# Seven gate and up tiles taken row by row, residual rows on VectorE alone, squares added by halves, and expert query rows made inside the second output projection

## The reference, cut to what matters

```
h = h + rmsnorm(hybrid_mixer(rmsnorm(h, g_pre_mix)), g_post_mix)
x = rmsnorm(h, g_pre_ffn)
g = causal_dwconv(x @ w_gate, w_conv)                # width 3 over tokens, D_FF = 5632
h = h + rmsnorm((silu(g) * (x @ w_up)) @ w_down, g_post_ffn)
# second block
p = rmsnorm_2(h, norm_mix_g) @ w_in                  # latents, keys, queries, gates
merged = gate_a * (o_a @ w_branch_a) + gate_b * (o_b @ w_branch_b)
h = h + merged @ w_out
h = h + peer_ffn(rmsnorm_2(h, norm_ffn_g))           # starts with x @ w_q, then top-k, experts
```

## Time and profile before

| | |
|---|---|
| median of the runs | 3484.07 us |
| profiled execution, its own time | 3487.23 us |
| its span, first to last instruction | 3485.4 us |
| TensorE (PE) busy | 3411.9 us, 98% |
| VectorE (DVE) busy | 2247.9 us, 64% |
| ScalarE (ACT) busy | 1644.5 us, 47% |
| GpSimd (POOL) busy | 120.7 us, 3% |
| HBM read | 586.71 MB, 170 GB/s |

### The profile page before, as it was taken

How to read it: one execution, slowest core, us unless ns; L and a number is a source line. 1 busy time by engine, 2 the same in 40 slices (tenths; PEclk the granted TensorE clock), 3 DMA queues, 4 the chain that set the end, 5 groups by cost and what they waited for, 6 DMA issues and landing times.

```text
span 3485.4 us, 60213 instructions
## 1 busy us (share of the span) xinstructions
PE 3411.9 (98%) x24920; PEld 3216.9 (92%) x24920; DVE 2247.9 (64%) x3715; ACT 1644.5 (47%) x2552; POOL 120.7 (3%) x173
## 2 busy tenths in 40 slices
PE   8999979999999989999999999999999999999998
PEld 8999979999999978999999999999999998887887
DVE  8775366666654467765575688877755555555655
ACT  5454444444444444444454544566644444444544
POOL 0000120000000020000000000022100000000000
PEclk9999989999999989999999999999999999999999
DMA  5433435555556634454565555544455555556654
GB/s 201 134 121 119 157 112 182 182 185 182 186 183 189 187 123 149 151 161 140 164 188 187 182 182 189 184 146 146 148 184 187 187 186 187 188 189 222 188 188 161
DMA packets 163712, 594.83 MB, mean 171 GB/s; under 512 B 18416, under 2 KB 19184, under 8 KB 163056
## 3 DMA queue, kind: packets, MB, share of 16 engines
q1 hardware_dynamic: 163440, 590.98, 53.0%
HBM read 586.71 MB, written 4.19 MB: 170 GB/s over the span
## 4 chain that ended last, share of the span: by engine, by line
PE 93%; DVE 4%; ACT 1%; DMA 1%; issue 0%; SPq 0%; ACTq 0%; DVEq 0%
PE ps L651 29%; PE ps L653 29%; PE ps L652 29%; PE ps L1086 2%; DVE wl L1158 1%; DVE tmp L1174 1%; PE ps L718 1%; ACT wh L1861 0%; DVE xl L1167 0%; PE ps L913 0%; DMA raw<-in_peer_v 0%; PE ps L894 0%; PE ps L760 0%; ACT xh L1867 0%; DVE ht L1190 0%
## 5 line engine op out<-in xcount | busy, mean ns | idle before, releaser
L1158 DVE TENSOR_TENSOR wl<-raw,wh 128x1024 fp32r<-128x1024 f32 x1114 | 1349.0, 1215 | 603.0 <-ACT wh L1861 599.9
L1861 ACT CAST wh<-raw 128x1024 fp32r<-128x1024 f32 x1114 | 1158.5, 1044 | 1029.0 <-PE ps L653 1025.6
L651 PE MATMUL ps<-xh,wh 128*128 128x256 f32 (+2 forms) x5248 | 1515.7, 289 | 47.6 <-DVE xl L1167 27.1
L653 PE MATMUL ps<-xh,wl 128*128 128x256 f32 (+2 forms) x5248 | 1496.3, 285 | 0.0
L652 PE MATMUL ps<-xl,wh 128*128 128x256 f32 (+2 forms) x5248 | 1494.4, 285 | 0.0
L651 PEld LDWEIGHTS ps<-xh,wh 128*128 128x128 f32 x5248 | 1005.8, 192 | 62.1 <-DVE xl L1167 18.3
L652 PEld LDWEIGHTS ps<-xl,wh 128*128 128x128 f32 x5248 | 1004.4, 191 | 2.3
L653 PEld LDWEIGHTS ps<-xh,wl 128*128 128x128 f32 x5248 | 1005.7, 192 | 0.0
L651 PE MATMUL ps<-wh,ch 128*128 128x512 f32 x1024 | 408.4, 399 | 0.6 <-DVE cl L1798 0.6
L653 PE MATMUL ps<-wh,cl 128*128 128x512 f32 x1024 | 403.4, 394 | 0.0
L652 PE MATMUL ps<-wl,ch 128*128 128x512 f32 x1024 | 401.6, 392 | 0.0
(11 more groups left out here) (339 smaller groups left out, 3163.2 us busy)
## 6 DMA issues: line engine op xcount, KB each, us to landing
raw<-in_peer_u SPq DMA_DIRECT2D x256, 512.0 KB, 4.2
raw<-in_peer_v SPq DMA_DIRECT2D x256, 512.0 KB, 4.4
raw<-in_w_in SPq DMA_DIRECT2D x208, 512.0 KB, 3.8
raw<-in_w_gate SPq DMA_DIRECT2D x88, 512.0 KB, 4.4
raw<-in_w_up SPq DMA_DIRECT2D x88, 512.0 KB, 4.6
raw<-in_w_down SPq DMA_DIRECT2D x80, 512.0 KB, 3.8
raw<-in_w_out SPq DMA_DIRECT2D x64, 512.0 KB, 4.3
raw<-in_w_branch_a SPq DMA_DIRECT2D x16, 512.0 KB, 3.6
```

Of the source, the lines that this page charges most:

```text
L651: t.matmul(o, lh, rh, start=start, stop=False)
L653: return t.matmul(o, ll, rh, start=False, stop=stop)
L1158: v.tensor_tensor(wl[:, i % SN, 0:cols(i)], raw[:, i % RN, 0:cols(i)], wh[:, i % SN, 0:cols(i)].bitcast(F32), ALU.subtract).then_inc(lo, 1)
L1861: s.copy(wh[:, i % SN, 0:cols(i)], raw[:, i % RN, 0:cols(i)]).then_inc(hi, 1)
```

## The change

It has five parts. The diff shows their core.

1. Gate and up tiles 0 to 6 get chunks of their own (`guk`): chunk k holds row k of all seven tiles, 128 x 896 numbers. TensorE takes the seven tiles together, 21 matmuls for each row, into seven banks; banks go round over eight instead of four. VectorE makes residual rows two ahead of the low rows. What is read from the finished tiles stands in a table `SIDESG` of slots (one slot per chunk) instead of behind every second chunk, and the first tap goes to ScalarE.
2. `post_row` does all rows on VectorE; GpSimd's `post_rows` is gone. Before the second input, the residual row k + 1 stands ahead of the low row k.
3. `sum_rows` adds the 16 squared rows as three additions of four rows and one of two, in place; TensorE sums the two rows left. This holds for all four norms of this kind.
4. ScalarE squares a finished tile before it copies it.
5. The high and low rows for the expert queries, and their squares, are made in the second output projection, each when its residual row is done. The first two expert query tiles are no longer taken as a pair.

```diff
-PLAN += _pairs("gu", 2 * FT)
+
+ROWS = 7
+PLAN += [("guk", k, 0) for k in range(KT)] + [("gu", n, c) for n in range(ROWS, 2 * FT) for c in range(2)]
...
-PLAN += _pairs("wq", 8)
+PLAN += [("wq", m, c) for m in range(8) for c in range(2)]
...
+def _sidesg():
+
+    at = [[] for _ in range(DN - GU + 8)]
+    b = KT
+    for f in range(FT):
+        b = max(b, 4 * f + 4 if f > 3 else 0)
+        if f == FT - 1:
+            b = 4 * f + 2
+        at[b] += [("g", f)]
+        at[b + 1] += [("conv", f)]
+        at[b + 2] += [("u", f), ("um", f)]
+        at[b + 3] += [("al", f)]
+        b += 2 if f % 2 else 1
+    return at
...
-        og = [ps[n % 4][:, 0:TQ if n % 2 == 0 else S] for n in range(2 * FT)]
+        def og(n):
+            return ps[n % 8][:, 0:TQ if n % 2 == 0 else S]
+
         xg = [halves(TQ), halves(S, 2)]
-        pair(GU, og[0:2], xg, 1)
-        for n in range(2, 2 * FT):
-            if n >= 4:
-                t.wait_ge(ev_gu, n - 3)
+        t.wait_ge(o_ev, 16)
+        for k in range(KT):
+            taken(GU + k)
+            t.wait_ge(xlo, 16 + k + 1)
+            for n in range(ROWS):
+                c = slice(128 * n, 128 * n + 128)
+                last = three(og(n), wh[:, (GU + k) % SN, c], wl[:, (GU + k) % SN, c], *xg[n % 2](k),
+                             k == 0, k == KT - 1)
+            last.then_inc(gemm, 1)
+            if k == KT - 2:
+                t.wait_ge(ms_add, 2)
+                mean_squares(ps[7][:, 0:TQ], [mt[:, 0, 0:TQ], mt[:, 1, 0:TQ]])
+        for n in range(ROWS, 2 * FT):
+            if n == 7:
+                t.wait_ge(ms, RMS.index("x2") + 1)
+            else:
+                t.wait_ge(ev_gu, READG.index(n - 8) + 1)
             for c in range(2):
-                chunk(GU + 2 * n + c, og[n], 8 * c, 8, xg[n % 2], c == 0, c == 1)
-            if n == 2:
-                t.wait_ge(ms_add, 4)
-                mean_squares(ps[7][:, 0:TQ], [tmp[:, 0, 0:TQ], tmp[:, 1, 0:TQ]])
+                chunk(AT["gu", n, c], og(n), 8 * c, 8, xg[n % 2], c == 0, c == 1)
...
-        pair(WQ, [ps[0][:, 0:S], ps[1][:, 0:S]], [x3, x3], 3)
-        for m in range(2, 8):
-            if m >= 4:
+        for m in range(8):
+            if m < 4:
+                t.wait_ge(res2, 12 + m + 1)
+            else:
                 t.wait_ge(qp_ok, m - 3)
             for c in range(2):
-                chunk(WQ + 2 * m + c, ps[m % 4][:, 0:S], 8 * c, 8, x3, c == 0, c == 1)
-            if m == 2:
-                t.wait_ge(ms_add, 8)
-                mean_squares(ps[7][:, 0:S], [tmp[:, 0, 0:S], tmp[:, 1, 0:S]])
+                chunk(WQ + 2 * m + c, ps[m % 4][:, 0:S], 8 * c, 8, x3, c == 0, c == 1,
+                      (lambda k: t.wait_ge(xlo, 48 + k + 1)) if m == 0 else None)
+                if (m, c) == (1, 0):
+                    t.wait_ge(ms_add, 4)
+                    mean_squares(ps[7][:, 0:S], [gate[:, 16, :], gate[:, 17, :]])
...
-        def half_sums(norm, sq_, T):
-
-            for g in range(2):
-                v.wait_ge(ms_sq, 4 * norm + 2 * g + 2)
-                v.tensor_reduce(tmp[:, g, 0:T], sq_[:, 8 * g:8 * g + 8, 0:T].rearrange("p k t -> p t k"), AX.X,
-                                ALU.add).then_inc(ms_add, 1)
+        def sum_rows(norm, rows, T, part):
+
+            if part < 3:
+                v.wait_ge(ms_sq, 4 * norm + part + 2)
+            if part:
+                v.wait_ge(own.sem, own.n)
+            if part < 3:
+                a, b = rows[:, 0:4, 0:T], rows[:, 4 * part + 4:4 * part + 8, 0:T]
+                v.tensor_tensor(a, a, b, ALU.add).then_inc(own.up(), 1)
+            else:
+                a, b = rows[:, 0:2, 0:T], rows[:, 2:4, 0:T]
+                v.tensor_tensor(a, a, b, ALU.add).then_inc(ms_add, 1)
...
-            if k % 2 == 0:
-                v.tensor_tensor(mt_[:, k, 0:T], mt_[:, k, 0:T], tmp[:, 4, 0:T], ALU.mult).then_inc(own.up(), 1)
-                v.wait_ge(own.sem, own.n)
-                v.tensor_tensor(ht[:, k, c0:c0 + T], ht[:, k, c0:c0 + T], mt_[:, k, 0:T], ALU.add).then_inc(res_v, 1)
+            v.tensor_tensor(mt_[:, k, 0:T], mt_[:, k, 0:T], tmp[:, 4, 0:T], ALU.mult).then_inc(own.up(), 1)
+            v.wait_ge(own.sem, own.n)
+            v.tensor_tensor(ht[:, k, c0:c0 + T], ht[:, k, c0:c0 + T], mt_[:, k, 0:T], ALU.add).then_inc(res_v, 1)
...
+        v.wait_ge(o_ev, 16)
+        post_row(0, mt, TQ, Q0)
+        post_row(1, mt, TQ, Q0)
+        low_row(1, 0, Q0, TQ, "g_pre_ffn")
+        post_row(2, mt, TQ, Q0)
+        low_row(1, 1, Q0, TQ, "g_pre_ffn")
+        for k in range(KT):
+            cut(GU + k + 2)
+            if k + 3 < KT:
+                post_row(k + 3, mt, TQ, Q0)
+            if k + 2 < KT:
+                low_row(1, k + 2, Q0, TQ, "g_pre_ffn")
+            if k in (6, 10, 13):
+                sum_rows(1, mt, TQ, (6, 10, 13).index(k))
+            if k == 13:
+                sum_rows(1, mt, TQ, 3)
+            if k == 14:
+                inverse_root("x2", ps[7][:, 0:TQ], D, EPS, rstd[:, 0:TQ])
...
-                v.tensor_scalar(c1, g1[:, 0:S], w[0], None, ALU.mult).then_inc(own.up(), 1)
-                v.wait_ge(own.sem, own.n)
+                v.wait_ge(gu_t, f + 1)
...
+        for slot in range(KT, DN - GU):
+            for name, f in SIDESG[slot]:
+                side_g(name, f)
             cut(GU + slot + 2)
...
+        v.wait_ge(o_ev, 32)
+        post_row(0, mt2, S, NM)
         for what, k in RAMP:
             if what == "x":
-                post_row(k, mt2, S, NM)
+                if k + 1 < KT:
+                    post_row(k + 1, mt2, S, NM)
...
+            if m:
+                low_row(3, m - 1, NM, S, "norm_ffn_g_2")
+            if m in (9, 13):
+                sum_rows(3, gate[:, 16:32, :], S, m // 4 - 2)
...
-            s.activation(mt_[:, m, 0:T], o, ACT.Copy, scale=pc(gain_name, m))
...
             s.activation(dst, o, ACT.Square).then_inc(o_sq, 1)
+            s.activation(mt_[:, m, 0:T], o, ACT.Copy, scale=pc(gain_name, m)).then_inc(o_ev, 1)
...
+        cut(GU + 2)
+        for k in range(-3, KT):
+            if k >= 0:
+                cut(GU + k + 3)
+            if k + 3 < KT:
+                s.wait_ge(res_v, k + 4)
+                high_row(1, k + 3, Q0, TQ, "g_pre_ffn")
+            if k in (0, 4, 8, 12):
+                squares_of(mt, Q0, TQ, k // 4)
+            if k == 14:
+                root("x2", rstd[:, 0:TQ])
...
+                s.wait_ge(ev_gu, READG.index(2 * f) + 1)
+                if f >= 2:
+                    s.wait_ge(gu_m, f - 1)
+                s.activation(c1, g_t[:, f % 2, 0:S], ACT.Copy, scale=pc("w_ffn_conv", 3 * f)).then_inc(gu_t, 1)
...
+        for m in range(16):
+            cut(O2 + 2 * m + 2)
+            cut(O2 + 2 * m + 3)
+            s.wait_ge(res2, m + 1)
+            high_row(3, m, NM, S, "norm_ffn_g_2")
+            if m == 3:
+                s.wait_ge(mg_l, 16)
+            if m % 4 == 3:
+                squares_of(gate[:, 16:32, :], NM, S, m // 4)
...
-        post_rows("post1", mt, TQ, Q0)
...
```

175 lines of the change are left out of this document (74 added, 101 removed).

## The result

The changed kernel takes 3455.88 us (median of four runs, 3451.66 to 3460.89), the kernel before 3483.91 (four runs, 3482.2 to 3485.85): ratio 0.992, 95% interval 0.9903 to 0.9937. The profiled execution took 3456.49 us, span 3453.8, 31.6 less than the span of before.

The account below looks back on a forecast made before the run. TensorE, busy 98% of the span, bounds the kernel; only its standstills and half-clock time can be won. Gains 2.2 + 20.2 + 5.9 + 5.0 = 33.3 us, from 3484.07, give 3451 us, range 3441 to 3464.

Parts of the forecast that it names:

- The start: At the kernel's start, TensorE's wait for sums goes as additions replace reductions: gain 2.2 us.
- B1: Between first output projection and down tiles: 31.4 us lost now, 11.2 after the change, gain 20.2 us.
- B2: After the down tiles: rows on VectorE alone, square first, quicker sums and earlier root gain 5.9 us, give or take 1.5.
- WQ: At the expert query tiles: waits for rows and sums and the half clock behind them go, gain 5.0 us.
- half clock: At the head of B1's rows, TensorE runs at 1.2 GHz after standing still: 2.0 us lost, from 1.4 to 2.6.
- square first: ScalarE squares before copying, so sums wait about 0.45 instead of 0.84 us at B1; gain 0.4 at B2.
- last pair: At the last gate and up tiles, TensorE waits 1.7 and 2.1 us for cuts: 3.8 us of new waiting.
- Catching up: After row 15 at B1, VectorE works off seven unread tiles by chunk 24: cost taken as 0, bounds 0 and 2 us.
- VectorE did not pace the rows: Rival at B1: VectorE paces the rows, 9.4 us more, 3460 us; chance 0.13.
- The clock came back in the row phase: Rival at B1: the clock does not come back in the row phase, 3480 us, no change; chance 0.06.
- The steady tiles: Rival in the steady gate and up tiles: late cuts cost 54 us over 37 pairs, 3505 us, slower; chance 0.04.
- The better case: Last-pair waits don't show and tables after B2 stop stalling, 3.8 + 3 us: 3444 us; chance 0.05.

Follow-up runs that it names:

- e5: Kernel before with VectorE making all 16 residual rows at B1 and B2, one row ahead of its low row, GpSimd none: 3475.02 us, ratio 0.9967.
- e6: Kernel before with the squared rows added by halves in place of two reductions, at all four places: 3475.67 us, ratio 0.9972.
- e7: Kernel before with both parts, e5 and e6, without seven tiles by rows or the expert rows' move: 3463.5 us, ratio 0.9938.
- e4: Changed kernel with unread matmuls added in the two long waits, 36 at B1 and 30 at B2: 3453.31 us, ratio 0.9911.
- e1: Changed kernel with the last gate and up pair read two chunks later and the root table loaded one chunk earlier: 3444.84 us, ratio 0.9883.
- e12: Changed kernel with the root table loaded one chunk earlier and nothing else: 3455.21 us, ratio 0.9916.
- e9: Kernel before with one wait added, TensorE starting the down tiles only when the last gate and up tile's low half is there: 3490.32 us, one run.

## Why the prediction was right, and where its steps were off

Forecast 3451 us, 33.3 less than the median of before; measured 3455.9, 28.0 less by the medians and 31.6 by the two profiled spans, inside the range. The start, B1, B2 and WQ all gave time. e5 and e6 show the residual rows and the additions one by one; what the rows of seven tiles and the move of the expert rows give is known only as the difference to e7. Part of how closely the sum fits is luck, as the terms show.

- **Start, 2.2 forecast:** 3.0 measured. The mechanism is as told; the matmuls from 25 to 45 us count more than the one wait. The remaining 1.8 of the 4.8 us at "out1" are no part of the change: the half clocks between 100 and 370 us differ from execution to execution (windows at 0.95 and 0.96), and put "out1" anywhere from 354.2 to 360.3 in kernels with the same code there. That the first down matmul came at 974.8, inside the 974 to 978 that I had named, is owed to this 1.8 as well.
- **B1, 20.2 forecast:** 17.5. Term by term: square first 0.48 for 0.45; row 0 at 4.99 for 4.95; half clock over 5.4 us (459.2 to 464.6), 2.4 lost for 2.0, which e4 took away and gained exactly; last pair 1.81 and 2.23 for 1.7 and 2.1; the 1.4 us of half clock behind it, which I had left to the range, did come (e1 gained 5.9 for both). Catching up cost nothing, as taken. That makes 13.3 lost in place of 11.2; 0.6 stays unassigned.
- **Down tiles, nothing forecast:** 2.9 lost. This is the step that failed: the sum has no term for them. I priced the wait at the last up tile as 2.1 us and looked no further than the clock; the matmuls behind it then ran 1.2% slower for 250 us. The wait alone doesn't fix that: e12 has it too, and lost 0.1 us there. The two waits cost 4.0 + 1.4 + 2.9 = 8.3 us in this execution. By the medians they cost more: e12 (3455.2) and e1 (3444.8) differ by the last pair alone, and that is 10.4 of e1's 11.0 us. That slower paces in the untraced runs of e12 make up the rest is argued.
- **B2, 5.9 forecast:** 6.4, by errors that cancel. Rows came every 1.19 us, not 1.31, so 5.4 us were saved instead of 3.75 (instructions of VectorE start 0.34 to 0.47 apart, and I had taken the longer figure for all three). The square first was to give 0.4 and lost 0.7: I had missed that the cast moved ahead leaves the table load right before the square. The order of ScalarE's instructions would have shown it. e12, with the table back, won 1.1 us there. And the wait for `gate` was 2.5 us in the trace of the changed kernel where it was 1.1 before: without these 1.4 us B2 would have given 7.8, so the match is luck in part, and some 1.4 us of gain stays without a term of mine.
- **WQ, 5.0 forecast:** 6.2. By e6 the additions alone give 4.3 of it, the wait for sums with the half clock behind it, and the move of the rows 1.9. In e9, with the code of before, the half clock was missing and WQ was 57.5, so 1.5 of the 6.2 depends on the execution.
- **Reduction against addition.** The Trainium skill, "VectorE: DVE Perf Modes", section "The perf-mode tier table (the rule you actually need)", puts both on one tier, from which the rival of e6 made 3483. e6 gave 3475.7. Here 2048 numbers, 8 rows reduced through a strided view, took 3.8 us, 1.87 ns each; an addition of 1024 took 3.88 / 3 = 1.29 us, 1.26 ns each. The measurement decides, and against that row of the table as it would apply here. Whether the reduction or its stride costs the time no run shows.
- **The rivals.** VectorE did not pace the rows (busy 94% of the phase, no wait; six rows neither). The clock came back in the row phase after 5.4 us. The steady tiles kept 0.1197 us. The better case, without the waits at the last pair, is e1: 3444.8 where I had written 3444. Its 3 us from tables that stop stalling did not come (the waits for `gate` in e1 are 4.6 us, 3.2 before); the pace of the down tiles and the half clock behind the waits made up for them, so that match is luck.

**The version to use** is e1: the change without the exception for the last pair and with the table loaded ahead of the last cast, 3444.84 us, ratio 0.9883 (0.9866 to 0.9899).

## What to carry to other kernels

When a step is moved behind a wait on an in-order engine, list what TensorE needs next that now stands behind it: an exception of two lines at one tile in 44 gave back a quarter of this change's gain. Count the work an engine does for the next stage in its program order, table loads included, not only the work of the stage itself. Compare stages, not only times: half clocks and paces that come and go moved single executions by 3 to 7 us, while the marks of a stage that no stop preceded agreed to 0.1 us.
